# A hybrid encoder step on one core: dense expert output over 512 prompt columns, gathered expert rows for 32 sample columns, and one program from the second residual on

## The reference, cut to what matters

```python
def block(xb):                                  # a block of 128 tokens
    qh = einsum('td,de->te', xb, w_pq).reshape(128, 8, 2, 128)
    s = einsum('thcd,hckd->thck', qh, sub_keys)
    sv, si = top_k(s, 16)
    cand = (sv[:, :, 0, :, None] + sv[:, :, 1, None, :]).reshape(128, 8, -1)
    cid = (si[:, :, 0, :, None] * 128 + si[:, :, 1, None, :]).reshape(128, 8, -1)
    top_s, top_pos = top_k(cand, 16)
    eid = take_along_axis(cid, top_pos)
    gate = softmax(top_s)
    act = gelu(einsum('thkd,td->thk', u_experts[eid], xb))
    return einsum('thk,thkd->td', gate * act, v_experts[eid])
```

## Time and profile before

| | us |
|---|---|
| median of 3 runs | 5138.51 (5134.13 to 5139.42) |
| the profiled execution, its own time | 5139.67 |
| its span, first to last instruction | 5137.6 |
| PE busy | 5002.0 (97%) |
| DVE busy | 2446.9 (48%) |
| POOL busy | 1311.7 (26%) |
| ACT busy | 1263.7 (25%) |
| DMA moved | 651.29 MB, mean 127 GB/s |

### The profile page before, as it was taken

The page is one execution under the profiler, slowest core; times in us unless marked ns, Lnnn a source line. Parts: engine busy times, 40 slices in busy tenths (PEclk is TensorE's granted clock), DMA queues, the critical chain, the costliest instruction groups (busy, mean ns, idle before and its releaser), DMA issues. The chain is left out here.

```text
span 5137.6 us, 92677 instructions
## 1 busy us (share of the span) xinstructions
PE 5002.0 (97%) x39028; PEld 4926.2 (96%) x39028; DVE 2446.9 (48%) x3653; ACT 1263.7 (25%) x1307; POOL 1311.7 (26%) x578
## 2 busy tenths in 40 slices
PE   8999899999989999999999999999999999999997
PEld 8999888899969999999999999999999999999997
DVE  4455545533222336776767677501444444444443
ACT  4233344322122222222111111112122122122122
POOL 0000122320001003343333333335233233233232
PEclk9999999999999999999999999999999999999998
DMA  3233432332342234333344444443333333333332
GB/s 149 100 126 117 152 105 94 106 121 90 135 148 82 95 110 161 120 122 104 126 136 152 136 152 136 152 156 144 142 119 139 142 121 137 142 122 136 142 124 76
DMA packets 233945, 651.29 MB, mean 127 GB/s; under 512 B 13696, under 2 KB 126720, under 8 KB 177024
## 3 DMA queue, kind: packets, MB, share of 16 engines
q1 hardware_dynamic: 233856, 650.03, 35.9%
HBM read 539.42 MB, written 110.56 MB: 127 GB/s over the span
## 5 line engine op out<-in xcount | busy, mean ns | idle before, releaser
L236 PE MATMUL pu<-xhi,whi 128*128 128x272 f32 x7456 | 1549.7, 289 | 38.3 <-DVE xlo L502 12.7
L236 PE MATMUL pu<-xhi,wlo 128*128 128x272 f32 x7456 | 1546.7, 289 | 0.0
L236 PE MATMUL pu<-xlo,whi 128*128 128x272 f32 x7456 | 1543.4, 289 | 0.0
L236 PEld LDWEIGHTS pu<-xhi,whi 128*128 128x128 f32 x7456 | 1176.0, 189 | 41.4 <-issue 36.3
L236 PEld LDWEIGHTS pu<-xlo,whi 128*128 128x128 f32 x7456 | 1176.2, 189 | 0.0
L236 PEld LDWEIGHTS pu<-xhi,wlo 128*128 128x128 f32 x7456 | 1169.5, 190 | 0.0
L220 ACT CAST whi<-raw 128x2048 fp32r<-128x2048 f32 x393 | 748.6, 1905 | 1528.2 <-PE pm L236 1183.7
L225 POOL TENSOR_TENSOR wlo<-raw,whi 128x2048 fp32r<-128x2048 f32 x128 | 606.6, 4739 | 1221.5 <-ACT whi L220 1221.5
L225 DVE TENSOR_TENSOR wlo<-raw,whi 128x2048 fp32r<-128x2048 f32 x265 | 610.5, 2304 | 396.7 <-ACT whi L220 388.6
L1480 POOL TENSOR_TENSOR clo<-coef,chi 128x544 fp32r<-128x544 f32 x124 | 261.8, 2132 | 994.4 <-ACT chi L1484 994.4
L1541 DVE TENSOR_TENSOR x<-pm,x 128x544 f32<-128x544 f32 x256 | 185.6, 725 | 584.0 <-PE pm L236 584.0
(11 more groups left out here) (298 smaller groups left out, 4903.2 us busy)
## 6 DMA issues: line engine op xcount, KB each, us to landing
raw<-units SPq DMA_DIRECT2D x393, 1024.0 KB, 4.9
h_s<-h_out SPq DMA_DIRECT2D x128, 272.0 KB, 2.1
gate_s<-table SPq DMA_DIRECT2D x17, 2048.0 KB, 9.5
h_in<-h_s SPq DMA_DIRECT2D x32, 1088.0 KB, 7.1
gate_in<-gate_s SPq DMA_DIRECT2D x32, 1088.0 KB, 9.1
q_s<-q_out SPq DMA_DIRECT2D x32, 320.0 KB, 2.2
x<-xT SPq DMA_DIRECT2D x8, 1088.0 KB, 6.8
qh<-q_s SPq DMA_DIRECT2D x8, 1088.0 KB, 7.3
```

The costliest lines, as they stand in the source:

```text
L236: ins = nc.tensor.matmul(out, w, xs[b][m == 1], start=(first and n == 0 and m == 0), stop=(last and n == len(terms) - 1 and m == 2))
```

## The change

In the output stage the dense product covers the 512 prompt columns only, as one pass of 512 columns into one PSUM bank. For the 32 sample tokens the 4096 pairs of token and expert are laid out as 32 slots of 128 rows. For each slot POOL issues 17 indirect DMAs (the hidden values, and 16 pieces of 512 bytes a row), DVE multiplies by gate and hidden value and adds into `row_sum`, and PE sums the four partitions of each token at the end. The gate tables shrink to 16 chunks. The blocks of the second residual, the hidden stage and the output stage become one. In DeltaNet the masks of levels 1 and up move from POOL into DVE's copy of the product, and the sample chunk's last operations cover 32 columns.

```diff
@@ residual_and_projection
-    def residual_and_projection(run, base, gain, split=None, first_head=None, renormalise=False):
+    def residual_and_projection(run, base, gain, split=None, first_head=None, experts=None):
...
                 ahead(base2, LAST, 0)
+                if experts:
+                    for k in range(KT - 4, KT):
+                        rescale(normal(k), k)
                 scale_out(LAST, 0)
                 ahead(base2, LAST, 1)
-                if renormalise:
-                    for k in range(KT - 4, KT):
-                        rescale(normal(k), k)
+                if experts:
                     for k in range(KT):
                         dve.wait_ge(renormed_hi, k + 1)
-                        nc.vector.tensor_tensor(xlo[:, k], normal(k), xhi[:, k].bitcast(F32), ALU.subtract)
+                        nc.vector.tensor_tensor(xlo[:, k], normal(k), xhi[:, k].bitcast(F32), ALU.subtract).then_inc(next_lo, 1)
                 scale_out(LAST, 1)
+                if experts:
+                    experts["vector"](dve)
...
-    TCH = T // TC
+    TCH = TP // TC
...
+    def dve_keep_slots(chain):
...
+        for g in range(P // TS):
+            ps, cs = slice(TS * g, TS * (g + 1)), slice(SLOTS * g, SLOTS * (g + 1))
+            v.tensor_copy(row[ps], flat(row_key)[ps, cs])
+            v.tensor_copy(col[ps], flat(col_key)[ps, cs])
+            ins = v.tensor_copy(slot_gate[ps], flat(gate)[ps, cs])
...
+        v.tensor_copy(slot_row, row_at)
+        v.tensor_copy(slot_at, h_at).then_inc(slots_kept, 1)
@@ hidden stage
+        for s in (0, 1):
+            sp.wait_ge(q_stored[s], 16 * KT + PRIME)
+        sp.dma_start(keys[:], a["keys"]).then_inc(keys_loaded, 16)
+        load_queries(0)
+        sp.dma_start(x_s, x[:]).then_inc(x_parked, 16)
...
+            def between(m, n):
+                if m == 0:
+                    pe.wait_ge(next_lo, 3 * KT + n + 1)
+                if (m, n) == (0, KT - 1):
+                    pe_scores(pe, t)
+                if turned and (m, n) == (STRETCH - 1, KT - 2):
+                    pe_turn(pe, t)
...
+        with pe.Fori(0, NCH - 1) as t:
+            stretch(t, True)
+        stretch(NCH - 1, False)
@@ output stage
+    first_slot = lambda group: min(2 * group, 8 + group)
+
+    def pool_rows(pool, group):
+
+        for j in range(first_slot(group), min(first_slot(group + 1), SLOTS)):
+            s = j % 2
+            if j >= 2:
+                pool.wait_ge(row_used, j - 1)
+            nc.gpsimd.indirect_dma_start(slot_h[:, j:j + 1], None, h_s.rearrange("k p (t o) -> (k p t) o", o=1),
+                                         bass.IndirectOffsetOnAxis(ap=slot_at[:, j:j + 1], axis=0)).then_inc(row_loaded[s], 16)
+            for o in range(KT):
+                nc.gpsimd.indirect_dma_start(rows[s][:, o], None, a["units"].rearrange("u p (t n) -> (u p t) n", n=P),
+                                             bass.IndirectOffsetOnAxis(ap=slot_row[:, j:j + 1], axis=0),
+                                             element_offset=o // 4 * (P * KT * P) + o % 4 * (GRP * P)).then_inc(row_loaded[s], 16)
+
+    def dve_row(dve, j):
+        s = j % 2
+        dve.wait_ge(row_loaded[s], 16 * (KT + 1) * (j // 2 + 1))
+        nc.vector.tensor_tensor(slot_h[:, j:j + 1], slot_h[:, j:j + 1], slot_gate[:, j:j + 1], ALU.mult).then_inc(slots_kept, 1)
+        dve.wait_ge(slots_kept, j + 2)
+        if j == 0:
+            ins = nc.vector.tensor_scalar(row_sum[:], rows[s][:], slot_h[:, j:j + 1], None, ALU.mult)
+        else:
+            dve.wait_ge(row_used, j)
+            ins = nc.vector.scalar_tensor_tensor(row_sum[:], rows[s][:], slot_h[:, j:j + 1], row_sum[:], ALU.mult, ALU.add)
+        ins.then_inc(row_used, 1)
+
+    def pe_sample(pe):
+        pe.wait_ge(row_used, SLOTS)
+        for k in range(KT):
+            ins = nc.tensor.matmul(pm[:, 0, 1, k * TS:(k + 1) * TS], row_sum[:, k], consts[:, C_SEL:C_SEL + TS], start=True, stop=True)
+        ins.then_inc(sample_out, 1)
...
-                    products([out_slot(d)[:, b, 0:HALF] for b in (0, 1)],
-                             [(whi[:, slot, GRP * d + k], wlo[:, slot, GRP * d + k], halves(chi[r], clo[r], k)) for k in range(GRP)],
+                    products([out_slot(d)[:, 0, 0:TP]],
+                             [(whi[:, slot, GRP * d + k], wlo[:, slot, GRP * d + k], [(chi[r][:, k], clo[r][:, k])]) for k in range(GRP)],
...
         for n in range(2 * VU):
+            group = 2 * i + n // VU - 1
+            if group >= 0 and n % VU in (0, 2):
+                for j in range(first_slot(group), min(first_slot(group + 1), SLOTS)):
+                    if j % 2 == n % VU // 2:
+                        dve_row(dve, j)
+            if last and n == 1:
+                dve_sample(dve)
...
         pool_coefs(pool, i * 2 + 1, 1, i + 1)
+        pool_rows(pool, 2 * i)
         if not last:
             pool_coefs(pool, i * 2 + 2, 0, i + 2)
+            pool_rows(pool, 2 * i + 1)
...
+    def experts_scalar(act):
+        hidden_stage_scalar(act)
+        finished(act, V0)
+        for q in range(GRP):
+            act_coef(act, 0, 0, q)
+        pairs(act, pair_act)
...
+    residual_and_projection(1, MO0, V_FFN, experts=dict(
+        sync=experts_sync, tensor=experts_tensor, scalar=experts_scalar, vector=experts_vector, gpsimd=experts_gpsimd))
@@ deltanet
-                    ins = nc.tensor.matmul(psum(D_)[:, h], L[l % 2][:, h], Tt[:, h], start=True, stop=True)
+                    ins = nc.tensor.matmul(psum(D_)[:, h], A[:, h], Tt[:, h], start=True, stop=True)
...
-                nc.scalar.copy(flat(half, b), bank(D_, b)).then_inc(q["level_pc"], 1)
...
+        for b in (0, 1):
+            level(dve, "level_x", c, 0, b)
+            tt(Tt[:, heads[b]], bc_h(ident), psum(A_)[:, heads[b]], ALU.subtract).then_inc(q["level_t"], 1)
         if ahead:
             dve_fill_split(dve, c, 1)
-        for l in range(levels):
+        for b in (0, 1):
+            tt(Tn[:, heads[b]], bc_h(ident), L[:, heads[b]], ALU.subtract)
+        for l in range(1, levels):
+            for b in (0, 1):
+                dve.wait_ge(q["level_p"], c * (2 * LEVELS - 2) + (2 * l + b - 1))
+                tt(half[:, heads[b]], psum(D_)[:, heads[b]], bc_h(consts[:, C_LEV + l * P:C_LEV + (l + 1) * P]), ALU.mult).then_inc(q["level_pc"], 1)
...
```

More of the change, by code:

```diff
@@ new lines, in hidden_stage_tensor, with stretch @@
+    def hidden_stage_tensor(pe):
+        def stretch(t, turned):
+            def between(m, n):
[5 more added lines that the diff above has]
+                    pe_turn(pe, t)
+            for m in range(STRETCH):
+                hidden_pe(pe, 0, STRETCH, t, m, before=lambda n: between(m, n))
+        with pe.Fori(0, NCH - 1) as t:
+            stretch(t, True)
+        stretch(NCH - 1, False)
+        with pe.Fori(0, TCH) as c:
+            for m in range(CHUNK_UNITS):
+                hidden_pe(pe, ROUTED, CHUNK_UNITS, c, m, before=lambda n: pe_quad(pe, c, 2 * m + n // 8) if n % 8 == 4 else None)
+        with pe.Fori(0, (P - TABLED) // 2) as i:
+            for m in (0, 1):
+                hidden_pe(pe, TABLED, 2, i, m)
@@ new lines, in hidden_stage_scalar, with hidden_stage_gpsimd @@
+    def hidden_stage_scalar(act):
+        with act.Fori(0, NCH) as t:
+            for m in range(STRETCH):
+                hidden_act(act, 0, STRETCH, t, m)
+                if m == STRETCH - 2:
+                    act.wait_ge(less_max, t + 1)
+                    nc.scalar.activation(ex[:], v2[:], ACT.Exp).then_inc(exped, 1)
+        with act.Fori(0, (P - ROUTED) // 2) as i:
+            for m in (0, 1):
+                hidden_act(act, ROUTED, 2, i, m)
+    def hidden_stage_gpsimd(pool):
+        with pool.Fori(0, P // 2) as i:
+            for m in (0, 1):
+                hidden_pool(pool, 0, 2, i, m)
+        pool_gate(pool, 0, 0, 1)
@@ L1464, in build @@
     VU = KT // 4
-    squares_before = counts["squares"]
-    counts["squares"] += KT
+    squares_before = counts["squares"] + KT
+    sums_before = counts["sums"] + 1
     place = region(HR, H_SIZE)
-    chi = [place(f"chi{i}", [GRP, T], F32R) for i in (0, 1)]
-    clo = [place(f"clo{i}", [GRP, T], F32R) for i in (0, 1)]
+    chi = [place(f"chi{i}", [GRP, TP], F32R) for i in (0, 1)]
+    clo = [place(f"clo{i}", [GRP, TP], F32R) for i in (0, 1)]
+    rows = [place(f"rows{i}", [KT, P]) for i in (0, 1)]
@@ L1844, in pe_chunk @@
             ready(pe, "sqo", c, b)
[L1845 removed]
+            nc.tensor.matmul(only(psum(C_), b, width), ones, only(sq, b, width), start=True, stop=True).then_inc(q["sso"], 1)
     eps = vecs[:, V_EPS:V_EPS + 1]
@@ L1982, in dve_chunk @@
                 chain.link(tt(Sd[:, hs], S[:, hs], bc_in(egam[:, hs, P - 1]), ALU.mult))
+            if l == 3:
+                for b in (0, 1):
+                    ready(dve, "att_done", c, b)
+                    tt(attm[:, heads[b]], att[:, heads[b]], bc_h(cum), ALU.mult)
             if ahead and l == 5:
```

(2 more changed lines are left out.)

373 lines of the change are left out of this document (189 added, 184 removed).

## The result

| | before | after |
|---|---|---|
| median, us | 5136.27 (5133.92 to 5140.8, 20 runs) | 5147.1 (5142.53 to 5151.36, 20 runs) |
| the profiled execution, us | 5139.67 | 5147.02 |
| its span, us | 5137.6 | 5145.2 |
| PE busy, us | 5002.0 | 4886.4 |
| POOL busy, us | 1311.7 | 1778.4 |

The ratio after to before is 1.0021 (1.0015 to 1.0027): a little slower, where 4984 us was forecast. PE has 116 us less to do, and the kernel still takes 11 us more. So PE must now stand still, and the stretches view of the changed kernel shows where. The columns are those of the earlier trace rows.

The account below looks back on a forecast made before the run. PE's passes were taken to bound the output and table stages, waits between engines DeltaNet. 5139.7 - 153 - 5.1 - 5 - 7 - 2.7 - 12 + 3.7 = 4958.6, plus 25 for POOL: 4984 us, range 4935 to 5095.

Parts of the forecast that it names:

- Dense output: Output stage: 6144 passes of 512 columns at 0.226 us each take 1389 us, a gain of 153 us.
- POOL's issues: Output stage, groups 0 to 7: at 1.0 us an issue, POOL needs 48.3 us a group, 4.9 over PE's; 25 us charged.
- I let it swallow 14 us: Output stage: coefficients made a group ahead absorb a first POOL lag of 14 us, a third of a group.
- 17 issues in groups 8 to 23, "up to 1.71": Output stage: 17 issues a group fit beside POOL's coefficients if one takes up to 1.71 us.
- Stage changes: Stage boundaries: gains of 7 us before the hidden stage, 5 at the tables, 2.7 at the output's start.
- DeltaNet: DeltaNet's four chunk heads: reordered DVE work and POOL's masks taken out gain 12 us, bounds 0 to 16.5.
- Trades the same two effects without fills; I leave it at 0: DeltaNet's sample chunk: shorter waits and DVE's added masked copy were traded against each other, change set at 0.
- POOL the bound, and slower: Output stage: issues of 1.57 us eat the whole gain, 1.8 us gives 5226 us; chance 0.11.
- DVE and POOL exclude each other: Output stage: DVE's splits and row sums hold POOL's issues, adding 13.8 us a group, so 5095 us; chance 0.15.
- three signs of being wrong: Waits far over 5 us each in the first eight groups, waits after group 8, or DeltaNet longer than 430 us.

Follow-up runs that it names:

- `late_use`: Changed kernel with slots from 16 on used by DVE at the third unit of the next group, not the first for even ones: 5117.06 us, ratio 0.9967.
- `even`: Changed kernel with its 544 issues spread evenly over groups 0 to 28, three row buffers and slots used at the next group's third unit: 5029.02 us, ratio 0.9795.
- experiment 5: Changed kernel with DVE's row sum made on one element a partition instead of 2048, for all slots but the first: 5099.35 us, ratio 0.9934.

## Why the prediction was wrong, point by point

**Dense output: right.** The pass was to start every 0.226 us and the stage to give 153; it starts every 0.2267, and the run without the sample part gives 147, most of the difference being those 0.0007 us a pass.

**POOL's issues: the step that failed.** "I take 1.0, nearer to the issue than to the pass" was the mis-sized term. An issue undisturbed holds POOL for 1.25 us, and for 50.6 / 34 = 1.49 in groups 1 to 8, where DVE's splits and row sums stretch some. The bounds of 0.39 to 2.13 held it, the value did not, nor did its reason, the 128 addresses: with 64 of them an issue still took 0.90 us. The group's coefficients were priced too high (14.3; they are 10.9 when POOL runs them in a row), which gave 3.4 back: 34 x 1.49 + 10.9 = 61.6 us, 18.1 over a group, where 4.9 were forecast.

**"I let it swallow 14 us": also failed.** Nothing was absorbed, and group 1 already lost 16 us. Made a group ahead is not due a group later: ACT takes the next group's `coef` in the first two units of this one, and the next unit's split stands behind it. I named the queues of DVE and POOL behind the added waits and left out ACT's, which handed on the lateness. 8 x 18.1 is 145, against 142 in the trace and a charge of 25.

**17 issues in groups 8 to 23, "up to 1.71": right as a capacity, wrong as a due time.** The even slot is wanted at the group's start, and 4.3 us of DVE's wait, 2.6 of its being held by POOL, and the row sum came together: 34 us in eight waits, of which `late_use` brought back 30.

**Stage changes: right in size, once for another reason.** The stop at the meeting before the hidden stage, 9.89 us in the earlier trace rows, is gone, and PE stands 3.08 us at the first scores instead; by the same pass eight units later 6.4 us are left as gain, 7 being forecast. That the 3 us agree is luck. They were charged for weights behind `x_s`; PE waits for the queries, of which the prediction said that they move up with the rest. They moved up 7.6 us, the first in the kernel before, the second after:

```profile
1927.30 0.43 SPq L1371 DMA_DIRECT2D qt<-q_s  x1
```

```profile
1919.75 0.66 SPq L1429 DMA_DIRECT2D qt<-q_s  x1
...
1927.97 5.46 PE L1273 MATMUL pm<-keys,qt 128*128 128x128 f32 x32 [3.08 <-DMA qt<-q_s]
```

PE's first pass of the stage moved up 13.8. The wait before the tables is gone. The one at the output is 1.95 (4.83 in the earlier trace rows), and the closing products take 3.65. At the final norm PE stands some 3 us longer than before, which I had not foreseen and did not follow up.

**DeltaNet: within the bounds for the chunks that I worked out, wrong in the one I set to 0.** The four prompt chunks gained 15.7 us by the starts of the chunks in the two traces; 12 were forecast. The sample chunk lost 10.7. "Trades the same two effects without fills; I leave it at 0" was the step: without fills there is no other work under DVE's queue, and PE's clock falls on top.

**The rivals.** *POOL the bound, and slower* is what happened; it had 0.11. Its threshold of 1.57 us an issue rested on the 14 us of absorption, on no loss after group 8 and on other gains of 181 us, of which 166 came; as things were, 1.49 was enough. *DVE and POOL exclude each other* was a part of it rather than an alternative. In that direction it cost 8 us a group (50.6 less 34 x 1.25), not 13.8, and the other direction, POOL's passes holding DVE's split, made the waits of 2.8 us that stayed in `even`. The Trainium skill, page "SBUF — State Buffer", section "SBUF: two separate sides", says that the pair is taken for a whole instruction and the other blocks; the trace agrees (0.94 us to 2.85 for an issue, 2.29 to 10.45 for a split), but for the nine issues of experiment 5 that begin with a split, and adds that DVE got no turn between six passes of POOL in a row.

Two of the three signs of being wrong that the prediction names came: waits far over 5 us in the first groups, and waits after group 8. With what was measured, 147 for the product, 26 for all stages ahead of it, 4 for the closing products, 3 at the final norm, and 142 and 34 for the two kinds of waits, the sum is 5139.7 - 147 - 26 + 4 + 3 + 142 + 34 = 5150, against the profiled 5147.

## What to carry to other kernels

When work moves to an idle engine, price one instruction of it from a run before planning the rate, and ask which engine takes that engine's other product, in which unit, and what stands behind the taking: an average of spare time says nothing about the due time. Spread such work evenly, and put the long passes of POOL apart from each other, since DVE can stand through a whole row of them. A stage without filler work needs its own order: what is harmless under other passes stops PE there, and the passes at half the clock after the stop (0.50 in the sample chunk) come on top.

## What the runs showed of the hardware that was not expected

- An indirect DMA on POOL has a nearly fixed price: 0.94 us busy and 0.30 to the next for 128 indices of 512 bytes, 0.95 for 1 KB pieces, 0.90 for 64 indices.
- DVE's operations with two SBUF inputs stretch POOL's issues: all 89 stretched issues of the changed kernel overlap a split or a row sum, and none of the 199 short ones beside DVE's additions, with one input from PSUM, is stretched. An issue hardly holds DVE in turn: the changed kernel's 50 splits beside issues and no POOL pass take 2.35 us at most, against 2.29.
- A DVE operation can be held through several POOL passes in a row: 10.45 us for a split of 2.29, through six passes.
- After a wait PE's passes here ran at half the granted clock for a while: some ten passes at 0.43 us after each wait of 15 us, some eight after six of the eight waits of 2.8 us, none after the other two. So the long wait costs 18 us, and the short one 4.7 or 3.1.
